# Feed-forward stages on unscaled x: norm factor applied to the sums, both parts of x in one 512-column operand, layers written out

## What is computed

```python
for l in range(2):                                     # first block
    x = x + 0.5 * swiglu(rmsnorm(x, ffn1_norm[l]), ...)      # FF = 2816
    u = rmsnorm(x, mix_norm[l]) @ w_in[l]                    # conv, rwkv, retention, mla mixers
    x = x + concat(y_conv, y_rwkv, y_ret, y_mla) @ w_out[l]
    x = x + 0.5 * swiglu(rmsnorm(x, ffn2_norm[l]), ...)
x = rmsnorm(x, final_norm)
h = x + pool_mixer(rmsnorm(x), ...)                    # second block
h = h + swiglu(rmsnorm(h), ...)                              # dense, FF = 2816
h = h + deltanet_mixer(rmsnorm(h), ...)
h = h + moe_ffn(rmsnorm(h), ...)                             # 8 experts, top 2, FF = 3584
return rmsnorm(h, final_norm)

def swiglu(x, w_gate, w_up, w_down):
    return (silu(x @ w_gate) * (x @ w_up)) @ w_down
def rmsnorm(x, g):
    return x * rsqrt(mean(x * x, -1) + eps) * g
```

## Time and profile before

| | us |
|---|---|
| median of 3 runs | 2869.95 (2867.29 to 2869.97) |
| profiled execution | 2867.51 |
| its span, first to last instruction | 2865.7 |
| PE busy / DVE busy / ACT busy | 2683.1 / 1906.5 / 1420.0 |
| mean granted TensorE clock | 0.977 |

### The profile page before, as it was taken

One profiled execution on the slowest core, in us unless ns is written; L12 is line 12 of the kernel. 1 busy time (PEld: TensorE's weight loads), 2 busy tenths in 40 slices (PEclk: granted clock), 3 DMA queues, 4 the chain that ended last, 5 costly groups with the idle time before them and its releaser, 6 DMA issues.

```text
span 2865.7 us, 49715 instructions
## 1 busy us (share of the span) xinstructions
PE 2683.1 (94%) x20030; PEld 2365.6 (83%) x20048; DVE 1906.5 (67%) x1722; ACT 1420.0 (50%) x1330; POOL 79.7 (3%) x82
## 2 busy tenths in 40 slices
PE   8999989999999989986999987999999999999997
PEld 7988888989988779976998986787777777787775
DVE  5456765555455855555546754788888888888786
ACT  4344513334344514343335733566766666666665
POOL 6000005000000000000000000000000000000000
PEclk9999999999999999997999999999999999999999
DMA  7564213555553305542555400899999999999995
GB/s 270 190 197 133 94 47 119 189 176 162 185 187 118 109 18 164 187 154 88 191 184 154 152 28 9 300 339 345 345 337 342 337 339 340 337 339 328 327 343 195
DMA packets 343044, 601.79 MB, mean 210 GB/s; under 512 B 12000, under 2 KB 180832, under 8 KB 342752
## 3 DMA queue, kind: packets, MB, share of 16 engines
q1 hardware_dynamic: 335264, 590.84, 60.7%
q10 hardware_dynamic: 7616, 8.58, 0.9%
HBM read 598.34 MB, written 1.05 MB: 209 GB/s over the span
## 4 chain that ended last, share of the span: by engine, by line
DMA 51%; PE 26%; DVE 11%; ACT 7%; DVEq 2%; issue 1%; SPq 1%; another core or an unknown queue 0%; ACTq 0%; PEldq 0%; PEld 0%; POOLq 0%
DMA raw<-in_moe_w_up 26%; DMA raw<-in_ffn_w_down 19%; DVE wlo L296 7%; ACT whi L293 6%; PE ps L430 5%; PE ps L792 5%; DMA raw<-in_dn_w_in 4%; PE ps L445 3%; DMA raw<-in_w_in 2%; PE ps L676 2%; PE ps L392 1%; DMA raw<-in_pool_w_in 1%; PE ps L1160 1%; PE ps L1147 1%; PE ps L1156 1%
## 5 line engine op out<-in xcount | busy, mean ns | idle before, releaser
L296 DVE TENSOR_TENSOR wlo<-raw,whi 128x2048 fp32r<-128x2048 f32 x562 | 1286.5, 2289 | 607.5 <-ACT whi L293 605.3
L293 ACT CAST whi<-raw 128x2048 fp32r<-128x2048 f32 x562 | 1071.6, 1908 | 677.5 <-DMA raw<-in_ffn_w_down 177.4
L430 PE MATMUL ps<-xhi,whi 128*128 128x256 f32 x1760 | 500.2, 284 | 3.2 <-DVE xlo L380 3.2
L430 PE MATMUL ps<-xlo,whi 128*128 128x256 f32 x1760 | 498.7, 283 | 0.0
L430 PE MATMUL ps<-xhi,wlo 128*128 128x256 f32 x1760 | 498.6, 283 | 0.0
L2499 PE MATMUL ps<-whi,xhi 128*128 128x512 f32 x896 | 365.3, 408 | 7.6 <-remote 5.6
L2499 PE MATMUL ps<-wlo,xhi 128*128 128x512 f32 x896 | 350.1, 391 | 2.9 <-issue 2.9
L2499 PE MATMUL ps<-whi,xlo 128*128 128x512 f32 x896 | 350.4, 391 | 0.0
L430 PEld LDWEIGHTS ps<-xhi,whi 128*128 128x128 f32 x1760 | 338.4, 192 | 5.8 <-DVE xlo L380 3.4
L430 PEld LDWEIGHTS ps<-xhi,wlo 128*128 128x128 f32 x1760 | 338.3, 192 | 1.9
L430 PEld LDWEIGHTS ps<-xlo,whi 128*128 128x128 f32 x1760 | 338.3, 192 | 0.0
(11 more groups left out here) (499 smaller groups left out, 3733.3 us busy)
## 6 DMA issues: line engine op xcount, KB each, us to landing
raw<-in_moe_w_gate SPq DMA_DIRECT2D x112, 1024.0 KB, 5.2
raw<-in_moe_w_up SPq DMA_DIRECT2D x112, 1024.0 KB, 5.5
raw<-in_moe_w_down SPq DMA_DIRECT2D x112, 1024.0 KB, 5.0
raw<-in_ffn_w_gate SPq DMA_DIRECT2D x55, 1024.0 KB, 5.1
raw<-in_ffn_w_up SPq DMA_DIRECT2D x55, 1024.0 KB, 5.1
raw<-in_ffn_w_down SPq DMA_DIRECT2D x55, 1024.0 KB, 4.8
raw<-in_w_in SPq DMA_DIRECT2D x24, 1024.0 KB, 5.1
raw<-in_dn_w_in SPq DMA_DIRECT2D x16, 1024.0 KB, 5.6
```

The costliest lines, as they stand in the source:

```text
L293: act.copy(whi[:, n % SPLIT, 0:width], raw[:, n % RAW, 0:width]).then_inc(hi_ready[n % SPLIT], 1)
L296: dve.tensor_tensor(wlo[:, n % SPLIT, 0:width], raw[:, n % RAW, 0:width], whi[:, n % SPLIT, 0:width], ALU.subtract).then_inc(split_ready[n ...
L430: mm = pe.matmul(dst[:, b * ntok:(b + 1) * ntok], w[:, n % SPLIT, c * GW + b * P:c * GW + (b + 1) * P], xt[part][:, c, 0:ntok], start=(c = ...
```

## The change

Four things are done together.

1. `xhi` and `xlo` become the two halves of one tensor `xboth`, so that for each weight block the high weights run once over 512 columns (high and low x side by side) and the low weights once over 256. Each 128-block of a tile now fills a bank of its own: gate in banks 4 and 5, up in 6 and 7 for every group. The sum of high weights on low x stands in columns 256 to 511 and is added afterwards: ACT copies it to SBUF, DVE adds the rest.
2. In the feed-forward stages x is turned unscaled, by transposes, piece by piece as it is added (`enter_tensor`). The norm factor is made beside the first gate tile, spread into a row over all partitions by two matmuls with ones (`row_tensor`), and multiplied into the gate sums before SiLU (`gate_sum`). The up sums stay unscaled, and the factor with the 0.5 or 1 stands as a scalar for each token in `add_y`. The other stages keep the norm they had.
3. The order on DVE and ACT in a group is new (below); the split of one tile moves into `add_y` behind its first addition.
4. The loop over layers is written out on every engine, gains are read from `vec` directly, and the stage `next` is gone; the final norm of the first block makes its own squares.

The diff, cut to its core:

```diff
-LAYER_PLAN = ['ffn1', 'mix_in', 'rwkv', 'out', 'ffn2', 'next']
+LAYER_PLAN = ['ffn1', 'mix_in', 'rwkv', 'out', 'ffn2']
...
-        xhi = sb("xhi", [P, C, S], F32R)
-        xlo = sb("xlo", [P, C, S], F32R)
+        xboth = sb("xboth", [P, C, 2, S], F32R)
+        xhi, xlo = xboth[:, :, 0, :], xboth[:, :, 1, :]
...
+        def enter_scalar(act, gain, splits=None):
+            act.activation(tiny[:, 72:73], small("one"), ACT.Sqrt)
+            if splits is None:
+                for i in range(len(PARTS) - 1):
+                    squares_of(act, i)
+            for s in range(2):
+                act.wait_ge(f["transposed"], s + 1)
+                if s == 1:
+                    act.sem_clear(f["transposed"])
+                for c in range(4 * s, 4 * s + 4):
+                    act.activation(xhi[:, c, :], turned_x(c, FFN_BANK), ACT.Copy, scale=gain(c)).then_inc(f["norm_hi"], 1)
+                if s == 0 and splits is None:
+                    squares_of(act, len(PARTS) - 1)
...
+            roots_of(act)
...
+        def enter_vector(dve, gain, scale, splits=None):
+            for c in range(C):
+                if c == 4 and splits is None:
+                    mean_vector(dve, 1)
+                dve.wait_ge(f["norm_hi"], c + 1)
...
+                dve.scalar_tensor_tensor(out=xlo[:, c, :], in0=turned_x(c, FFN_BANK), scalar=gain(c), in1=xhi[:, c, :],
+                                         op0=ALU.mult, op1=ALU.subtract).then_inc(f["xt_ready"], 1)
...
+            take(dve, f["root"])
+            dve.reciprocal(tiny[:, 6:6 + TT], tiny[:, 10:10 + TT])
+            dve.drain()
+            for t in range(TT):
+                dve.tensor_scalar(turn[:, t, :], const("ident"), tiny[:, 6 + t:7 + t], None, ALU.mult)
+            dve.tensor_scalar(tiny[:, 12:12 + TT], tiny[:, 6:6 + TT], scale, None, ALU.mult)
+            dve.drain().then_inc(f["scaled"], 1)
...
+        def enter_tensor(pe):
...
+            pe.wait_ge(f["x_part"], 1)
+            for c in range(4):
+                turn_block(0, c)
+            pe.wait_ge(f["x_part"], 2)
+            for c in (4, 5):
+                turn_block(0, c)
+            pe.wait_ge(f["x_part"], 3)
+            for c in range(4):
+                tr = turn_block(1, c)
+            tr.then_inc(f["transposed"], 1)
+            pe.wait_ge(f["x_part"], 4)
+            for t, c in ((0, 6), (0, 7), (1, 4), (1, 5), (1, 6), (1, 7)):
+                tr = turn_block(t, c)
+            tr.then_inc(f["transposed"], 1)
...
-        def wide(pe, n, dst, ntok, xt, fresh=False):
+        def wide(pe, n, first_bank):
             take_split(pe, n)
             for b in range(2):
                 for c in range(C):
-                    if fresh and b == 0:
-                        wait_xt(pe, c)
-                    for k, (w, part) in enumerate(PASSES):
-                        mm = pe.matmul(dst[:, b * ntok:(b + 1) * ntok],
-                                       w[:, n % SPLIT, c * GW + b * P:c * GW + (b + 1) * P],
-                                       xt[part][:, c, 0:ntok], start=(c == 0 and k == 0),
-                                       stop=(c == C - 1 and k == 2))
+                    pe.matmul(ps[:, first_bank + b, :], whi[:, n % SPLIT, c * GW + b * P:c * GW + (b + 1) * P],
+                              xboth[:, c].rearrange("p a t -> p (a t)"), start=(c == 0), stop=False, skip_group_check=True)
+                for c in range(C):
+                    mm = pe.matmul(ps[:, first_bank + b, 0:S], wlo[:, n % SPLIT, c * GW + b * P:c * GW + (b + 1) * P],
+                                   xhi[:, c, :], start=False, stop=(c == C - 1), skip_group_check=True)
             return mm
...
+            wide_fresh(pe, n, GATE_BANK).then_inc(tile_done[n % SPLIT], 1)
+            row_tensor(pe)
+            wide(pe, n + 1, UP_BANK).then_inc(tile_done[(n + 1) % SPLIT], 1)
+            take(pe, f["row_taken"])
+            open_y(pe, 2 * TT)
...
             def gate(m, q):
                 take(act, tile_done[m % SPLIT])
-                act.activation(sil[:, q, 0:w], ps[:, 4 + q, 0:w], ACT.Silu)
+                act.copy(two(sil[:, q, :]), two_parts(GATE_BANK)[1]).then_inc(gate_copied, 1)
+                split_hi(act, m + SPLIT)
+                take(act, gate_summed)
+                act.activation(sil[:, q, :], sil[:, q, :], ACT.Silu)
+
+            def up(m):
+                take(act, tile_done[m % SPLIT])
+                act.copy(two(hid), two_parts(UP_BANK)[1]).then_inc(up_copied, 1)
                 split_hi(act, m + SPLIT)
...
             def step(m, q):
+                refill(m - 1 + SPLIT)
+                gate_sum(q)
                 refill(m + SPLIT)
+                up_sum()
+                make_hidden(q)
                 refill(m + 1 + SPLIT)
-                hid_group(q)
-                refill(m + 2 + SPLIT)
-
+            row_vector(dve)
+            gate_sum(0)
+            refill(n + 2)
+            up_sum()
             refill(n + SPLIT)
-            refill(n + 1 + SPLIT)
-            hid_group(0)
+            make_hidden(0)
...
-        def add_y(dve, scale):
+        def add_y(dve, scale, after_first=lambda: None):
             for i, (t, s) in enumerate(PARTS):
+                if i == 1:
+                    after_first()
...
-            with long_loop(eng, DEPTH) as l:
-                n = 0
+            n = 0
+            for l in range(DEPTH):
+                now["layer"] = l
```

More of the change, by code:

```diff
@@ L371, in scale_vector, with norm_vector @@
                                   ALU.mult).then_inc(f["scaled"], 1)
-        def norm_vector(dve, gain, first, known=False):
-            if not known:
-                scale_vector(dve)
+        def norm_vector(dve, gain, first):
+            scale_vector(dve)
             for c in range(C):
@@ new lines, in enter_scalar @@
+        def enter_scalar(act, gain, splits=None):
[11 more added lines that the diff above has]
+                    squares_of(act, len(PARTS) - 1)
+            if splits is not None:
+                splits(act)
+                for i in range(len(PARTS)):
+                    squares_of(act, i)
+            roots_of(act)
@@ new lines, in row_tensor, with row_vector @@
+        def row_tensor(pe):
+            take(pe, f["scaled"])
+            pe.sem_clear(f["x_part"])
+            pe.wait_ge(consts_rest, 16)
+            for t in range(TT):
+                mm = pe.matmul(ps[:, 0, t * P:(t + 1) * P], const("ones"), turn[:, t, :], start=True, stop=True)
+            mm.then_inc(f["row_made"], 1)
+        def row_vector(dve):
+            take(dve, f["row_made"])
+            dve.tensor_copy(turn.rearrange("p t m -> p (t m)"), ps[:, 0, 0:S])
+            dve.drain().then_inc(f["row_taken"], 1)
@@ L2788, in build, with add_ffn, is_first @@
         STREAM, TENSOR, VECTOR, SCALAR, POOL = {}, {}, {}, {}, {}
-        def add_ffn(part, gain, names, scale, in_layers, known=False):
+        def add_ffn(part, gain, names, scale, in_layers):
+            def is_first(n, l):
+                return part == "ffn1" and l == 0
             def stream(sp, n, l):
@@ L2942, in _ @@
             pool.wait_ge(f["pos_in"], 16)
-            with pool.Fori(0, DEPTH) as l:
+            for l in range(DEPTH):
                 for part in LAYER_PLAN:
```

155 lines of the change are left out of this document (89 added, 66 removed).

## The result

The changed kernel takes 2830.4 us (median of 4 runs, 2826.5 to 2831.9) against 2869.4 for the kernel before beside it; the ratio is 0.9861, 95% interval 0.9849 to 0.9873. The forecast was 2830.0 (2812 to 2849). The total came out to half a microsecond, and part of that is luck: a gain of 7.2 us and losses of 12.1 us that stand nowhere in the working cancel for the most part.

What follows compares the result with a forecast made beforehand. PE was taken to bound the feed-forward stages, DMA the untouched expert stage. 21.1 + 5.4 + 7.5 + 4.1 + 0.9 + 3.2 - 2.1 = 40.1 us off the 2869.95 median gave 2830, range 2812 to 2849.

Steps and rivals of the forecast that it cites:

- The matmuls: Gate and up in feed-forward groups: one 512 and one 256 column matmul replace three of 256, saving 21.1 us.
- The rival without a gain: Gate and up matmuls: a 256-column matmul behind a 512 pays back the saving; 2851 us, chance 0.11.
- The added work: Feed-forward groups: ACT's extra copies and DVE's extra sums stay hidden behind PE, with 5.8 us of cover; cost 0.
- The slower rival: Feed-forward groups: sums arrive too late, so PE waits for the next gate tile's split; 2896 us, chance 0.05.
- The rival with more gain: Gate and up matmuls: 256 columns at 0.114 us, plus cheaper code loading; about 2810 us, chance 0.08.
- The entries: Five entries: turning x unscaled and loading final-norm gains earlier save 5.4, 7.5, 4.1, 0.9 and 3.2 us.
- Layer turn: Layer 0 to layer 1: the gate starts sooner after the last down matmul, net 7.5 us.
- Final norm: First block's final norm: its gains are loaded earlier because the stage next is gone, saving 3.2 us.
- Cold entries: Projection entries and layer turn: the gate tile starts at 1.2 GHz, costing 5.5 us; 2835 us, chance 0.14.
- The exits: Mixer and delta-net entries: the split behind the first addition makes the last addition 0.7 us later, 2.1 us lost.
- The written-out layers: Layer loop written in line: only 1.3 us booked, inside the layer turn; bound 4.5 us either way.
- new gaps in the second layer: Sign of being wrong: gaps in the second layer where the first has none; no size given.

Runs made afterwards that it cites:

- e4_three: The changed kernel with three passes of 256 columns in place of 512 and 256: 2870.0 us, ratio 0.9994.
- f2_dve_act_pad: The changed kernel with 144 empty instructions on DVE and 10 on ACT in the pool stage: 2830.1 us, ratio 0.9861.
- e5_refill_first: The changed kernel with the split of the next stage's second tile ahead of the first addition to x, as before: 2838.0 us, ratio 0.9892.
- f3_hidden_first: The kernel before with only the hidden tile made ahead of the split, plus a signal from ACT: 2868.7 us, ratio 0.9990.
- e2_both: The kernel before with only the 512 and 256 column matmuls and the new order in a group: 2849.9 us, ratio 0.9929.
- g2_late_pad: g1_late with 144 empty instructions on DVE, spread over pool stage and pool projection, and 10 on ACT: 2817.8 us, ratio 0.9819.
- g1_late: The changed kernel with the next stage's second-tile split behind the next norm at four exits (not layer 0 to 1): 2828.4 us, ratio 0.9855.

## Why the prediction was right, and where it was not

**The matmuls (21.1 us): right.** 55 groups x (16.98 - 16.61) = 20.4 us, and going back to three passes puts a group at 16.98 again. This rested on two durations from one chain, 0.228 and 0.120 us. The rival without a gain falls. The 39.6 us of e4_three would by themselves say that the matmuls are worth twice as much; only the traces, stage by stage, keep them apart from the place of the code.

**The added work (0): right.** In the groups, PE waits for nothing: two of them take 33.22 us at three places running. The slower rival, sums that come too late, falls with it. The rival with more gain, 256 columns at 0.114 us, falls as well: a group isn't below 16.61.

**The entries: right in size.** Projection to second feed-forward: PE's gate follows the last down matmul after 2.50 us instead of 5.33 and, in layer 1, 2.49 instead of 5.14; the row costs 0.36 (446.89 to 447.25), so 4.8 us together (forecast 5.4). Layer turn: 2.72 us instead of 10.55, 7.5 with the row off (7.5). Pool mixer: the gate follows PE's last matmul there after 7.09 us instead of 13.28, the first tile takes 6.64 us where it takes 5.70 at the higher clock, and the row is off; that leaves 4.9 (4.1). Start: 0.5 (0.9), what is left of the 6.0 at the end of that stage after eleven groups and the last down tile. Final norm: PE's gap 7.79 instead of 10.87, 3.1 (3.2).

**Cold entries: the rival falls.** The first gate matmul at the projection and the layer entry takes 0.50 us against 0.78 where PE is slow, the granted clock is 1.00 from the transposes on, and the first tile takes 5.70 to 5.79 us. The Trainium skill's rule ("TensorE: Matmul & The Clock Gate", Part 4: PE-mode transpose), that transposes do not count as busy for the clock, was weighed against this change. A run decides more than the forecast could. In f2_dve_act_pad PE stood idle for 7.32 us, did nothing but 16 transposes, at a granted clock of 0.50, and then ran the gate tile at the higher clock from its first matmul (granted clock 0.98 from 1313 to 1314 us, 1.00 behind it):

```profile
1309.99 3.59 PE L438 MATMUL ps<-con,x 128*128 128x128 f32 x16 [7.32 <-DVE x L1889]
1313.49 0.50 PE L518 MATMUL ps<-xboth,whi 128*128 128x512 f32 x1
```

In the changed kernel, with an idle time of 3.45 us ahead of the same transposes, the gate was slow for another 2 us. So transposes don't keep the clock down here, and for these transposes of float32 the measurement decides against the rule.

**The exits (-2.1 us): the size of a part was right, its reason wrong, and the rest missing.** The step said that the split behind the first addition makes the others 0.7 us late. The gaps did grow by 0.75, 0.73 and 0.82 us. But e5_refill_first, the other order, is 7.6 us slower. What made the gaps grow is that PE now arrives 1.45 us earlier: it no longer waits for the hidden tile. That wait stood in the trace of before, five times 1.45 us, 7.2 in all, and the forecast had read the end of a stage on DVE only from 204 us on, just behind it. The lesson is in f3_hidden_first: taking the wait away alone gave 1.5 us in the median, hardly more than a measurement can tell, as the next wait took it over and lowered the clock as well.

**The written-out layers: a term too small, and in the wrong place.** The bound of 4.5 us was read from a stop at the loop turn, and alone the edit gave 9.3 us by the medians; its trace shows 5.3 at the turn and 4.0 in the expert stage. The forecast held that stage to be untouched, "so that stays at its length". No instruction of it changed and yet its length lay between 1085.2 us (e2_both) and 1110.6 (e4_three). In the changed kernel it was 5.9 us longer than before.

**The sum.** The terms measured: 20.4 + 4.8 + 7.5 + 4.9 + 0.5 + 3.1 - 2.3 (exits) = 38.9, where 40.1 were forecast. Not forecast: +7.2 for the last down tiles, and against it -5.9 in the expert stage, -4.7 in the mixers of layer 1 and -1.5 at the first mixer (its slow norm). That is 34.0; the traces have 35.7, and 1.7 us are not placed. Of the 4.7 in layer 1, 1.65 us is one group of 16 matmuls that ran at the lower clock this time (7.03 us, 5.38 before), and 1.6 lie at the end, of which 1.3 are stops of PE:

```profile
889.03 7.03 PE L984 MATMUL ps<-work 96*128 96x256 f32 x16 [3.37 <-DVE U L1158]
...
983.91 1.27 PE L1482 MATMUL ps<-U,work 64*64 64x64 f32 x37 [1.03 <-issue]
```

The prediction named new gaps in the second layer as a sign of being wrong, and these are such: 0.30 us at 977.29 and 1.03 at 983.91, each behind a 16 KB packet of q8 that ended 1.5 and 1.4 us before, so the term for written-out code has a small loss in it too. The last 1.5 us of the 4.7 is the second part of the projection. Its first matmuls, behind a gap of 2.28 us, stand 0.12 us apart in layer 1 of the kernel before (granted clock 1.00) and 0.21 us in its layer 0 (0.50). Of the 28 such stretches in the 14 traces, 26 took 26.1 to 26.6 us and two 24.7; one of the two is this one. So two thirds of the 4.7 is the clock, which fell well in the trace of before and badly in the one of after. The forecast of 2830 was met because +7.2 and -12.1 cancel but for 4.9 and because it was made against the median; its own terms were good to about 1 us of 39, and the rest was outside its model. The range of 37 us was wide enough for them, for other reasons than those given.

## What to carry to other kernels

Read the last group of a stage and the first of the next as closely as the steady state: a wait there is hidden in no average, and when it is taken away the next one in line (here the norm, behind a split that nobody needed yet) has to be moved too, or it takes the gain and lowers the clock. Put work on the engine that ends the chain behind what the chain waits for, even a microsecond of it. When kernels with loops are compared, compare them stage by stage: code that only moved made a stage without an edit 25 us longer or shorter, more than most edits; a few empty instructions in idle time are a cheap way to find out, and g2_late_pad, 12.6 us faster than the changed kernel (and 51.5 faster than the one before), is partly that.

## What the runs showed of the hardware

- The spacings of 0.228 us for 512 columns and 0.120 for 256 hold when the two widths take turns by eights: 16 of each make a tile, 5.57 us by the sum and by the trace (11.14 for gate and up).
- At the turn or the end of a loop an engine can stop for 6.2 to 6.7 us (PE), 6.5 to 6.6 (DVE) or 4.4 to 5.9 us (ACT), or for about 1 us or not at all, by how many instructions stand ahead of the loop. A packet of the instruction queues ends 1.2 to 1.9 us before the engine goes on. 192 empty instructions on PE cost 23 us in all.
- The clock after a short idle time isn't a function of its length alone. After 2.65 us the same 32 matmuls took 5.44 us at the first mixer and 3.81 at the second in the changed kernel, and in f2_dve_act_pad the other way round (3.81 and 5.30). In the 14 traces, after 1.44 to 2.05 us they took 3.8 to 4.3 us every time, after 3.27 us or more 5.2 to 6.8 every time, and in between the one or the other.
- One profiled execution isn't the median: g1_late's took 2823.4 us, 5 below the median of its five. A difference of 5 us between two kernels is therefore read from the medians, and the trace only tells its place.
